# Layer 0's MLP products formed from seven block products each, with its modulation sums on TensorE

## The reference

```python
D_MODEL, SEQ, CTX_LEN, DEPTH = 1024, 512, 256, 2      # D_FF = 4 * D_MODEL, N_MOD = 6
...
def squared_relu_mlp(h, w1, w2):
    return jnp.square(jax.nn.relu(h @ w1)) @ w2
...
def hybrid_layer(x, xc, mod, mod_c, p, cos, sin, ctx_out):
    sh1, sc1, ga1, sh2, sc2, ga2 = jnp.split(mod[:, None, :], N_MOD, axis=-1)
    ...
    h = rms_norm(x, p['g_norm1']) * (1.0 + sc1) + sh1
    z = jnp.split(h @ p['w_in'], offs, axis=-1)
    ...
    y = jnp.concatenate([o_a, o_b, o_c, o_d], axis=-1) @ p['w_out']
    x = x + ga1 * y
    x = x + ga2 * squared_relu_mlp(rms_norm(x, p['g_norm2']) * (1.0 + sc2) + sh2, p['w_mlp1'], p['w_mlp2'])
    if ctx_out:
        ...
        xc = xc + ga2c * squared_relu_mlp(rms_norm(xc, p['g_norm2']) * (1.0 + sc2c) + sh2c, p['w_mlp1'], p['w_mlp2'])
    return x, xc
...
    for l in range(DEPTH):
        mod = s_c @ w_mod[l] + b_mod[l]
        mod_c = s_cc @ w_mod[l] + b_mod[l]
```

## Time and profile before

| what | value |
|---|---|
| median of 3 runs | 2021.47 us |
| profiled execution, device time | 2017.82 us |
| its span in the trace | 2016.0 us |
| TensorE busy | 1845.9 us, 92% |
| VectorE busy | 1081.2 us, 54% |
| ScalarE busy | 700.9 us, 35% |
| GpSimd busy | 529.6 us, 26% |
| granted TensorE clock, mean | 0.963 |

### The profile page before, as it was taken

One profiled execution on the slowest core, in us unless ns is written; L12 is line 12 of the kernel. 1 busy time (PEld: TensorE's weight loads), 2 busy tenths in 40 slices (PEclk: granted clock), 3 DMA queues, 4 the chain that ended last, 5 costly groups with the idle time before them and its releaser, 6 DMA issues.

```text
span 2016.0 us, 28541 instructions
## 1 busy us (share of the span) xinstructions
PE 1845.9 (92%) x11692; PEld 1543.3 (77%) x11692; DVE 1081.2 (54%) x1719; ACT 700.9 (35%) x941; POOL 529.6 (26%) x156
## 2 busy tenths in 40 slices
PE   5899998879877999999999979999788979999998
PEld 3788896568766888888888868878567758787776
DVE  3384836567337766857757854853566652222122
ACT  4433257543205212212212236234763353222230
POOL 0224512000211221222222222362200324434342
PEclk8899999999987999999999999999899989999999
DMA  8421112000131223332323223111200012222221
GB/s 324 173 105 43 64 42 105 1 1 1 63 125 63 106 104 127 118 113 100 112 103 125 105 92 125 64 63 43 105 1 1 32 60 97 85 103 83 104 84 63
DMA packets 23906, 172.84 MB, mean 86 GB/s; under 512 B 2628, under 2 KB 3050, under 8 KB 4842
## 3 DMA queue, kind: packets, MB, share of 16 engines
q1 hardware_dynamic: 23786, 171.09, 23.0%
HBM read 162.69 MB, written 8.39 MB: 85 GB/s over the span
## 4 chain that ended last, share of the span: by engine, by line
PE 73%; issue 7%; DVE 7%; ACT 7%; DMA 2%; POOL 2%; SPq 1%; DVEq 0%; POOLq 0%; ACTq 0%
PE ps L1720 46%; PE ps L1892 7%; PE ps L1707 5%; POOL w_lo L471 1%; PE ps L1974 1%; DMA raw<-w_big 1%; PE ps L1690 1%; PE ps L1825 1%; DMA raw<-w_modl 1%; PE ps L2020 1%; DVE mx L1396 1%; ACT tmp L638 1%; PE ps L2027 1%; PE ps L2052 1%; PE ps L2055 1%
## 5 line engine op out<-in xcount | busy, mean ns | idle before, releaser
L471 POOL TENSOR_TENSOR w_lo<-raw,w_hi 128x2048 fp32r<-128x2048 f32 x96 | 445.0, 4636 | 1155.0 <-ACT w_hi L581 1155.0
L581 ACT ACTIVATE w_hi<-raw 128x2048 fp32r<-128x2048 f32 x96 | 183.1, 1908 | 394.2 <-PE ps L1720 356.6
L1720 PE MATMUL ps<-h_hi,w_hi 128*128 128x512 f32 x880 | 265.9, 361 | 0.1
L1720 PE MATMUL ps<-h_lo,w_hi 128*128 128x512 f32 x880 | 260.9, 356 | 0.0
L1720 PE MATMUL ps<-h_hi,w_lo 128*128 128x512 f32 x880 | 260.8, 355 | 0.0
L1050 DVE SCALAR_TENSOR_TENSOR mod_acc<-raw,cs,mod_acc 128x256 f32<-128x256 f32 x392 | 251.2, 709 | 0.0
L1720 PE MATMUL ps<-hid_hi,w_hi 128*128 128x512 f32 (+1 forms) x768 | 234.3, 359 | 0.0
L1720 PE MATMUL ps<-hid_lo,w_hi 128*128 128x512 f32 (+1 forms) x768 | 232.9, 357 | 0.0
L1720 PE MATMUL ps<-hid_hi,w_lo 128*128 128x512 f32 (+1 forms) x768 | 232.9, 357 | 0.0
L1538 DVE SCALAR_TENSOR_TENSOR xT<-ps,modall,xT 128x512 f32<-128x512 f32 x120 | 75.4, 657 | 285.2 <-PE ps L1720 280.4
L1564 DVE TENSOR_TENSOR tmp<-tmp 128x768 f32<-128x768 f32 (+1 forms) x64 | 67.0, 1049 | 193.0 <-ACT tmp L914 192.6
(11 more groups left out here) (298 smaller groups left out, 3080.7 us busy)
## 6 DMA issues: line engine op xcount, KB each, us to landing
raw<-w_big SPq DMA_DIRECT2D x96, 1024.0 KB, 4.8
raw<-w_modl SPq DMA_DIRECT2D x40, 1024.0 KB, 4.8
first_mod<-w_modl SPq DMA_DIRECT2D x8, 1024.0 KB, 19.2
x_keep<-xT SPq DMA_DIRECT2D x2, 3072.0 KB, 10.9
xT<-x_keep SPq DMA_DIRECT2D x2, 3072.0 KB, 10.5
xin<-x_in SPq DMA_DIRECT2D x4, 512.0 KB, 7.9
out<-xout SPq DMA_DIRECT2D x4, 512.0 KB, 2.7
xin<-ctx_in SPq DMA_DIRECT2D x2, 512.0 KB, 9.9
```

The lines of the kernel that those rows point to most:

```text
L471: nc.gpsimd.tensor_tensor(w_lo[r][:], raw[raw_r][:], w_hi[r][:].bitcast(F32), ALU.subtract).then_inc(sem("lo_ready"), 1)
L581: nc.scalar.activation(w_hi[w % 2][:], raw[raw_of(w)][:], ACT.Copy).then_inc(sem("hi_ready"), 1)
L1720: ins = mm(pair(g, a, b - a), w[:, k, m * P:(m + 1) * P], mov[hl][:, k, a:b], start=(k == 0 and q == 0), stop=(k == KD - 1 and q == 2))
```

## The change

**Blocks.** In layer 0 each quarter's two products, 1024 x 1024 on 768 tokens, are cut in halves in all three directions: four 512x512 blocks of weights (`11`, `12`, `21`, `22`), 384 tokens, half of the input features. Instead of eight block products, seven are made, by Strassen's scheme in Winograd's form. For them VectorE forms four sums of weight blocks (`s1`, `s2_s4`, `s3`) and four of operand halves (`t_sum`) for each of the two products. A block product (a phase, `P_` 0 to 6 for the hidden, 7 to 13 for the output) is 2 x 24 matmuls, 384 wide; `c_` is its half (two groups of 128 features). Some products pile up in PSUM on earlier ones, in banks 0 to 3 or (`Y_PHASES`) 4 to 7. ScalarE keeps a copy of three intermediate sums and VectorE adds it (`past_sums`, `evict`); output products are added to `xT` as they come.

**High and low halves.** The weights' high parts are made by ScalarE in chunks of 128x1024 (`high_w`), the low parts by VectorE (`low_w`), no longer by GpSimd. Operands' high and low parts are one operation each, 128x1536 (`high_a`, `low_a`). Weights land in `raw[0]`, `raw[1]` and two more buffers (`raw21`, `raw22`), modulation slots in a fifth (`raw_m`).

**Modulation.** `mod_sum` and `mod_slot` are gone. All slots go through TensorE's row products: 8 at the start as before, 7 in layer 0's input projection (6 before), 8 in its output projection (6), 12 in its MLP (28), 7 in layer 1's input projection and 6 in its output projection (none). For that, layer 1's projections use `raw[1]` for `w_mod` and have only `raw[0]` for weights; both are used from `MLP_1` on.

**Norms.** Ahead of layer 0's MLP the normalised stream is kept in fp32 (`h_mlp`), written in halves of 384 tokens (`norm_mlp`); ScalarE takes the root for both halves first. Ahead of layer 1's input projection the squares are summed in two halves too. `split_hi` of layer 1's second slot moves from before to behind the norm's loop.

```diff
--- before.py
+++ after.py
...
+PROJ = IN_SLOTS + OUT_SLOTS
+LAYER_SLOTS = PROJ + QUARTERS * 2 * BLOCKS
+PHASES = 14
...
+MOD_AT = ((0, 0), (1, 0), (2, 0), (2, 1), (3, 0), (3, 1), (4, 0))
+IN_MODS = len(MOD_AT)
+OUT_MODS = (8, 6)
+Q_MODS = 3
...
-MOD_AT = ((0, 0), (1, 0), (2, 0), (2, 1), (3, 0), (3, 1))
...
+Y_PHASES = (1, 2, 5)
+FRESH = (0, 1, 2)
+PAST_SUMS = (1, 4, 5)
...
+                if w == PROJ:
+                    sp.wait_ge(sem("mw_lo"), 2 * PHASES * (QUARTERS - 1) + 24)
+                elif w == MLP_1 + 1:
                     sp.wait_ge(sem("mod_summed"), DEPTH * MOD_SLOTS - FIRST_MODS)
+                elif w > MLP_1:
+                    sp.wait_ge(sem("lo_ready"), wts.at(-1))
                 elif w > 0:
-                    sp.wait_ge(sem("lo_ready"), wts.at(0 if w < ONE_RAW else -1))
+                    sp.wait_ge(sem("lo_ready"), w)
                 sp.dma_start(raw[raw_of(w)][:], idx).then_inc(landed(w)[0], 16)
                 wts.add()
+
...
+                        if part == 1:
+                            mod(1)
+                            mod(2)
+                            if last:
+                                break
+                        sp.wait_ge(sem("mw_sum"), sums.at(8 * part + 4))
+                        load_block("21", *to)
+                        sp.wait_ge(sem("mw_lo"), los.at(PHASES * part + 10))
+                        load_block("11", *to)
+                        sp.wait_ge(sem("mw_lo"), los.at(PHASES * part + 12))
+                        load_block("12", *to)
+                        sp.wait_ge(sem("mw_lo"), los.at(PHASES * part + 14))
+                        load_block("22", *to)
+                        if part == 1:
+                            mod(3)
+                    sums.add(16)
+                    los.add(2 * PHASES)
+
+                looped = [(sums, 16), (los, 2 * PHASES), (mods, Q_MODS)]
...
-                if x_total == 0:
-                    split_hi(1)
+                if which == 1:
+                    split_hi(l * PROJ + 1)
...
+            def high_w(P_, c_):
+
+                p, r, part = P_ % 7, P_ % 2, P_ // 7
+                if p in (0, 1, 6):
+                    name = {0: "11", 1: "12", 6: "22"}[p]
+                    act.wait_ge(tile_landed(name), landed_n.at(16 * (part + 1)))
+                    src = chunk(mlp_raw[name], c_)
+                else:
+                    act.wait_ge(sem("mw_sum"), sums.at(8 * part + {2: (3, 4), 3: (5, 7), 4: (1, 2), 5: (6, 8)}[p][c_]))
+                    src = chunk(w_sum[r], c_) if p in (2, 3) else chunk(mlp_raw[{4: "11", 5: "12"}[p]], c_)
+                act.wait_ge(sem("big_done"), big.at(2 * (P_ - 2) + c_ + 1))
+                nc.scalar.activation(chunk(w_hi[r], c_), src, ACT.Copy).then_inc(sem("mw_hi"), 1)
+
...
+                for P_ in range(PHASES):
+                    if P_ + 1 < PHASES or not last:
+                        high_w(P_ + 1, 1)
+                    past_sums(P_ - 1, 1)
+                    done = 8 if P_ == 10 else P_ - 1
+                    if norm_next and P_ != 9 and done in LAST_OF_X:
+                        square_x(done, 0)
+                        square_x(done, 1)
+                    if P_ == 0 and not first or 7 <= P_ < 13 or P_ == 13 and not last:
+                        high_a(P_ + 1)
+                    if P_ < 6:
+                        high_a(P_ + 2)
+                    if P_ + 2 < PHASES or not last:
+                        high_w(P_ + 2, 0)
+                    past_sums(P_, 0)
+                if norm_next:
+                    split_hi(PROJ)
+                    square_x(13, 0)
+                    nc.scalar.activation(tbl[:, 0:1], eps[:], ACT.Ln)
+                    rstd(slice(HALF, T), bank(5, 0, HALF))
+                    square_x(13, 1)
+                    T_("acc").add(6)
...
-            def mod_sum(half):
-
-                if half == 0:
-                    dve.wait_ge(sem("mod_landed"), sum_n.at(1) * 16)
-                    dve.wait_ge(sem("mod_used"), sum_n.at(FIRST_MODS))
-                for k in range(4 * half, 4 * half + 4):
-                    for c_i in range(2):
-                        if k == 0:
-                            ins = v.tensor_scalar(mod_acc[:, c_i, :], raw[1][:, k, :], cs[:, k, c_i:c_i + 1], None,
-                                                  ALU.mult)
-                        else:
-                            dve.wait_ge(sem("dve_step"), own.at(-1))
-                            ins = v.scalar_tensor_tensor(mod_acc[:, c_i, :], raw[1][:, k, :], cs[:, k, c_i:c_i + 1],
-                                                         mod_acc[:, c_i, :], ALU.mult, ALU.add)
-                        if (k, c_i) != (KD - 1, 1):
-                            ins.then_inc(sem("dve_step"), 1)
-                            own.add()
...
+                def s2_s4(part, c_):
+                    dve.wait_ge(sem("big_done"), big.at(PHASES * part + 2 + c_ + 1))
+                    dve.wait_ge(sem("mw_sum"), sums.at(8 * part + 2))
+                    s2 = chunk(w_sum[1 - part], c_)
+                    v.tensor_tensor(s2, chunk(raw22, c_), chunk(raw[0], c_), ALU.subtract).then_inc(sem("mw_sum"), 1)
+                    dve.wait_ge(sem("mw_sum"), sums.at(8 * part + (5, 7)[c_]))
+                    dve.wait_ge(sem("mw_lo"), los.at(PHASES * part + 2 + c_ + 1))
+                    at = chunk(raw[1], c_)
+                    v.tensor_tensor(at, at, s2, ALU.subtract).then_inc(sem("mw_sum"), 1)
+
...
+                for P_ in range(PHASES):
+                    part, p = P_ // 7, P_ % 7
+                    after = P_ + 1 if P_ + 1 < PHASES or not last else None
+                    if P_ >= 1:
+                        evict(P_ - 1, 1)
+                    if P_ == 8:
+                        mod_result(0)
+                    if p == 1:
+                        s1(part, 1)
+                    elif p == 2:
+                        s2_s4(part, 1)
+                        t_sum(l, n_t, part, 3)
+                    elif p == 4:
+                        t_sum(l, n_t, part, 4)
+                    if P_ == 7:
+                        t_sum(l, n_t, 1, 1)
+                    if after is not None:
+                        low_w(after, 0)
+                    if P_ == 8:
+                        mod_copy(rows)
+                    if P_ == 0 and not first or P_ >= 7 and after is not None:
+                        low_a(l, n_t, P_ + 1)
+                    if p == 0:
+                        t_sum(l, n_t, part, 2)
+                    if P_ < 6:
+                        low_a(l, n_t, P_ + 2)
+                    if P_ == 7:
+                        mod_copy(rows)
+                    if after is not None:
+                        low_w(after, 1)
...
+                    evict(P_, 0)
+                    if P_ == 12 and not last:
+                        t_sum(l, n_t, 0, 1, 1)
+                    if P_ == 13:
+                        mod_result(1)
+                        mod_copy(rows)
+                    if p == 0:
+                        s1(part, 0)
+                    elif p == 1:
+                        s2_s4(part, 0)
+                evict(13, 1)
+                mod_result(2)
+                if norm_next:
+                    add_sq(7, 0, 0)
...
-                        if l == 0:
-                            mod_rows_sum()
+                        mod_rows_sum()
                         continue
                     for m in range(2):
                         k = 2 * s + m
                         pe.wait_ge(sem("x_done"), T_("xd").n - 1)
                         feature_group(k, r, m, (yT_hi, yT_lo), n_t)
                         T_("xd").add()
-                        if l == 0:
+                        if k < OUT_MODS[l] + 2:
                             mod_columns()
-                            if k < 2 * OUT_SLOTS - 1:
...
+            def product(P_, n_t):
+
+                h = n_t // 2
+                p, r, ra = P_ % 7, P_ % 2, P_ % 3
+                base = 4 if p in Y_PHASES else 0
+                ops = (op_hi[ra], op_lo[ra])
+                w3 = ((w_hi[r], 0), (w_hi[r], 1), (w_lo[r], 0))
+
+                def term(g, k):
+                    for q, (w, hl) in enumerate(w3):
+                        ins = mm(bank(base + g, 0, h), wide(w)[:, k, g * P:(g + 1) * P], ops[hl][:, k, 0:h],
+                                 start=(p in FRESH and k == 0 and q == 0), stop=(k == 3 and q == 2),
+                                 skip_group_check=True)
+                    return ins
+
+                for c_ in range(2):
+                    pe.wait_ge(sem("mw_lo"), wlo.at(2 * P_ + c_ + 1))
+                    if P_ in (1, 8) and c_ == 1:
+                        pe.wait_ge(sem("mod_out"), mods_out.at(1))
+                        if P_ == 8:
+                            pe.wait_ge(sem("mod_copied"), copies.at(1))
+                    if P_ in (0, 1):
+                        pe.wait_ge(sem("x_done"), xd.at((-1, -3)[P_] + c_))
```

(34 more changed lines are left out.)

695 lines of the change are left out of this document (515 added, 180 removed).

## The result

The changed kernel takes 2009.11 us (median of 4 runs, 2006.18 to 2010.30), the one before 2022.32 (4 runs, 2019.67 to 2023.76): ratio 0.9934, 95% interval 0.9917 to 0.9951. It is faster by 13 us, not by the 47 forecast, and lies outside the range of 1948 to 2006.

The account below looks back on a forecast made before the run. TensorE was taken as the bound; -52 (three quarters) - 12 - 16 + 1.4 + 21 + 11 = -46.6 us on the profiled 2017.8 gave 1971, and 1975 us as median (3.65 higher), range 1948 to 2006.

Parts of the forecast that it names:

- The bound, the matmuls: Layer 0's MLP: TensorE bounds it, 384-wide matmuls take 0.1776 us each, TensorE alone 123.6 us a quarter.
- 2.1 us are lost, I take 2.4: 126 us a quarter: Layer 0's MLP: TensorE's waits on VectorE's order in phases 8 to 11; a quarter 126 us against 143.3.
- First quarter and norm: Layer 0's MLP norm and first quarter: 12 us less, with phase 1 waiting on VectorE's queue.
- phase 1 waits for `low_w`: First quarter: low weights stand behind `t_sum` on VectorE until 635.5, while phase 0 ends at 627.
- Layer 0's output projection: Three row products' waits for modulation loads mostly go, less one more slot's 1.4 us: -16 us.
- Layer 0's input projection has one more: +1.4: Layer 0's input projection: one additional modulation slot through TensorE's row products costs 1.4 us.
- Seven row products in the input projection ... 10.0: Layer 1's input projection: TensorE-bound row products cost 10.0 us; with waits +21 us, ends 10 and 35.
- the late split and the load: Layer 1's input projection: 3.4 us wait for the second slot's weights; 5.3 for a modulation load, plus 3 of clock.
- Layer 1's output projection and norm: Output projection +11 us, from six row products at 8.6 and a load wait of 2; norm 0.
- D: Rival: MLP gains, but layer 1's modulation is dear and layer 0's output projection keeps its waits: 2007 us; chance 0.05.
- A: Rival in layer 0's MLP: VectorE becomes the bound, about 133 us a quarter, 2003 us; chance 0.13.
- B: Rival in layer 0's MLP: serial handshake adds 4.2 us per affected phase; with five, 147 a quarter, 2059 us; chance 0.08.

Follow-up runs that it names:

- GpSimd in pieces: GpSimd's low half of a weight tile as 4 operations of 512 columns: with the seven edits 1958.89 us, alone on the changed kernel 2007.76 us.
- the seven edits: Changed kernel with earlier copy, split and last square, both MLP order edits, both norms' roots regrouped, product 1's second weight low half earlier: 1964.66 us, ratio 0.9715.

## Why the prediction was wrong

Point by point, by its own steps; they account for the 34.8 us between -46.6 and the -11.8 of the profiled execution.

- **The bound, the matmuls: right.** 0.1776 us taken, 0.1777 measured; TensorE 123.6 and 123.45 busy. The columns/2.4 + 2.5 ns that the prediction sets against its rows stands in the same section of the Trainium skill ("TensorE: Matmul & The Clock Gate", Back-to-back issue gap) as "the *isolated* single-MM gap"; the prediction leaves that condition out.
- **"2.1 us are lost, I take 2.4: 126 us a quarter":** 4.0 lost, 127.6. Right in kind: the waits for `low_a` and the residual, ahead of phases 10 and 11, were named. That of 1.5 us for the eviction ahead of product 2 was missed, since the walk began at the end of phase 6. The three quarters gave 46, not 52. The cut of VectorE's work showed that TensorE bounds them.
- **First quarter and norm: -12 forecast, -7.2 measured.** The mis-sized term is what stands behind "phase 1 waits for `low_w`": product 0 was late too, and the eviction of product 1 (5.1 us) wasn't counted. That VectorE's queue sets the stage was right.
- **Layer 0's output projection: right**, -19.3 (-17 by the middle of nine profiles) for -16. No wait for `raw<-w_modl` is left between 536 and 594 us.
- **"Layer 0's input projection has one more: +1.4": the step that failed.** It took a row product at TensorE's price and put the wait for its copy at nothing, without asking what stands ahead of the copy on VectorE. The price was 11.7 us; moving the copy alone gave 8.5 back, the 7.8 us of wait with some of the lower clock behind it. The 1.4 itself was good: in the later kernels with the copy early the stage took 121.1 to 124.1 us, 1.2 to 4.2 over before.
- **"Seven row products in the input projection ... 10.0": the same error again, in layer 1.** The whole was priced at 21 and took 35.4. The waits that were foreseen, the late split and the load, were real: 2.1 and 5.7 us with slow clock; the early split gave 9 us back, against 3.4 + 5.3 + 3 forecast. The 10.2 us for the copy was not foreseen; moving the copy alone gave 7. Of the 14.4 us that the price was short here, 7 are thus shown to be the copy's, and the rest is open.
- **Layer 1's output projection and norm: right**, 13.1 for 11 and 0.3 for 0.

Two terms, the row products of the two input projections, thus miss 25 of the 35 us, and two of the MLP are short by 5 and 6; layer 0's output projection gave 3 more than forecast. The omission of the copy's place, at both, is shown for 15.5 of the 25. Of the rivals D came nearest in time (2007), by luck: it has the 35 us of layer 1's input projection without a reason for them, and the waits it kept in layer 0's output projection went. A and B, the MLP's own, didn't come. Shown by experiment: the copy's place, the split's place, TensorE's bound in the quarter. Not shown: what the 2.8 us are that stay in layer 0's input projection once the copy is early (124.1 against 119.9, less 1.4 for the row product); with the same order there other kernels had 121.1 to 123.7. Open: how the 188.7 us to layer 1's output projection's end divide; it varies by 8 us between profiles.

With the order mended the change is worth what had been forecast, and more: 1964.7 us, or 1958.9 with GpSimd in pieces. By stages, the profile of the seven edits against the one before has -52 us for the three quarters (forecast -52), -14 for norm and first quarter (-12), -16.5 for layer 0's output projection (-16), +1.4 for its input projection (+1.4), +12 for layer 1 up to the attention (+21) and +14 up to its output projection's end (+11). Waits that the forecast counts (in the quarters, and 11 of the 21 us) are in part mended there, so this is not the prediction come true.

## What to carry to other kernels

When a small step is put at a new place in a program, price it on every engine that takes part, by what stands ahead of it in that engine's queue at that time: here 1.4 us of TensorE's work cost 8.5 more, because its 0.4 us copy stood behind 19 us of other work, most of it scans. A long wait in a profile may be free, and removing it then only shows the next; move one thing, and read the end of the stage, not the wait. Where a schedule is walked, begin the walk at the stage's first instruction, since half of a quarter was walked here and the largest missed wait lay in the other half.
